# High and low parts of stationary weights stored as alternating words of one tile

## What is computed

```python
def swiglu(h, w_gate, w_up, w_down):
    return (jax.nn.silu(h @ w_gate) * (h @ w_up)) @ w_down

for l in range(DEPTH):
    h = rms_norm(x, ffn1_norm[l])
    x = x + 0.5 * swiglu(h, ffn1_w_gate[l], ffn1_w_up[l], ffn1_w_down[l])
    h = rms_norm(x, mix_norm[l])
    proj = h @ w_in[l]                     # 1024 -> 3080 columns
    # dilated window attention (4 heads of 64), multiscale pooling (256 channels),
    # gated DeltaNet (4 heads of 128, short convolution, chunks of 64)
    ...
    x = x + jnp.concatenate([ya, yb, yc], axis=-1) @ w_out[l]
    h = rms_norm(x, ffn2_norm[l])
    x = x + 0.5 * swiglu(h, ffn2_w_gate[l], ffn2_w_up[l], ffn2_w_down[l])
return rms_norm(x, final_norm)
```

## Time and profile before

| | before |
|---|---|
| median of three runs | 1030.73 us |
| the three runs | 1030.73, 1031.29, 1030.73 us |
| span of the profiled execution | 1029.2 us |
| TensorE busy | 1018.1 us, 99%, 6482 matmuls |
| TensorE weight loads busy | 887.9 us, 86% |
| VectorE busy | 738.5 us, 72% |
| ScalarE busy | 603.0 us, 59% |
| GpSimd busy | 210.0 us, 20% |
| read from HBM | 175.05 MB |

### The profile page before, as it was taken

One profiled execution on the slowest core, in us unless ns is written; L12 is line 12 of the kernel. 1 busy time (PEld: TensorE's weight loads), 2 busy tenths in 40 slices (PEclk: granted clock), 3 DMA queues, 4 the chain that ended last, 5 costly groups with the idle time before them and its releaser, 6 DMA issues.

```text
span 1029.2 us, 19004 instructions
## 1 busy us (share of the span) xinstructions
PE 1018.1 (99%) x6482; PEld 887.9 (86%) x6482; DVE 738.5 (72%) x1204; ACT 603.0 (59%) x1101; POOL 210.0 (20%) x248
## 2 busy tenths in 40 slices
PE   9999999999999999999999999999999999999996
PEld 7888888899988888888888888889999888888885
DVE  6677666798776866666777666678986877666665
ACT  6555555776655655555675555558675575555554
POOL 2867111100400211111111111110014003111111
PEclk9999999999999999999999999999999999999999
DMA  7966666584124666666747666665732238666661
GB/s 246 281 201 188 185 192 190 138 247 153 63 63 123 192 197 187 193 190 184 205 136 211 184 184 188 192 171 164 226 103 66 88 95 266 185 189 196 184 184 41
DMA packets 249881, 176.79 MB, mean 172 GB/s; under 512 B 5875, under 2 KB 235400, under 8 KB 249704
## 3 DMA queue, kind: packets, MB, share of 16 engines
q1 hardware_dynamic: 248800, 174.35, 57.2%
q0 software_dynamic: 400, 1.43, 0.4%
q10 hardware_dynamic: 632, 0.34, 0.1%
HBM read 175.05 MB, written 1.05 MB: 171 GB/s over the span
## 4 chain that ended last, share of the span: by engine, by line
PE 95%; DVE 2%; ACT 2%; issue 0%; DVEq 0%; POOL 0%; POOLq 0%; ACTq 0%
PE bank L742 30%; PE bank L745 16%; PE bank L726 13%; PE bank L727 13%; PE bank L728 13%; PE bank L786 1%; PE bank L1138 1%; PE bank L1125 1%; PE bank L1061 1%; PE bank L751 1%; ACT big L1455 1%; DVE X L1894 1%; PE bank L793 1%; ACT X L1462 1%; DVE Wl L1852 0%; ACT L1567 0%
## 5 line engine op out<-in xcount | busy, mean ns | idle before, releaser
L1852 DVE TENSOR_TENSOR Wl<-raw,Wh 128x1024 fp32r<-128x1024 f32 x324 | 413.8, 1285 | 77.7 <-ACT Wh L1391 77.6
L1391 ACT ACTIVATE Wh<-raw 128x1024 fp32r<-128x1024 f32 x323 | 330.5, 1054 | 84.1 <-PE bank L728 82.2
L742 PE MATMUL bank<-X,Wh 128*128 128x512 f32 x1344 | 336.8, 393 | 0.0
L742 PEld LDWEIGHTS bank<-X,Wh 128*128 128x128 f32 x1344 | 246.8, 188 | 48.9
L745 PEld LDWEIGHTS bank<-X,Wl 128*128 128x128 f32 x1344 | 182.9, 189 | 14.3 <-DVE Wl L1852 0.3
L609 POOL TENSOR_TENSOR gact<-gact,pooled 128x256 f32<-128x256 f32 x85 | 73.8, 868 | 575.7 <-DVE gact L1951 567.1
L745 PE MATMUL bank<-X,Wl 128*128 128x256 f32 x1344 | 187.2, 282 | 0.0
L726 PE MATMUL bank<-Wh,aH 128*128 128x512 f32 x336 | 132.9, 395 | 0.0
L727 PE MATMUL bank<-Wl,aH 128*128 128x512 f32 x336 | 131.9, 392 | 0.0
L728 PE MATMUL bank<-Wh,aL 128*128 128x512 f32 x336 | 131.5, 391 | 0.0
L1506 ACT ACTIVATE dec<-bank 128x256 f32<-128x256 f32 x88 | 33.6, 382 | 118.6 <-PE bank L745 118.5
(11 more groups left out here) (319 smaller groups left out, 1291.7 us busy)
## 6 DMA issues: line engine op xcount, KB each, us to landing
raw<-in_ffn_w_gate SPq DMA_DIRECT2D x88, 512.0 KB, 3.8
raw<-in_ffn_w_up SPq DMA_DIRECT2D x88, 512.0 KB, 3.7
raw<-in_ffn_w_down SPq DMA_DIRECT2D x88, 512.0 KB, 4.3
raw<-in_w_in SPq DMA_DIRECT2D x48, 512.0 KB, 4.3
raw<-in_w_out SPq DMA_DIRECT2D x16, 512.0 KB, 3.5
cst<-in_consts POOLq DMA_DIRECT2D x1, 1200.0 KB, 6.2
xr<-in_x SPq DMA_DIRECT2D x2, 512.0 KB, 4.2
out_x<-big SPq DMA_DIRECT2D x3, 256.0 KB, 2.7
```

The source lines that it names most:

```text
L742: nc.tensor.matmul(b[:, :], piece(Wh, s)[:, k, :], X[:, k, :, :], start=k == 0, stop=False)
L1391: return nc.scalar.activation(Wh[:, s, 0:D_MODEL], raw[:, s, :], ACT.Copy).then_inc(hi_cast.sem, 1)
L1852: return nc.vector.tensor_tensor(Wl[:, s, 0:D_MODEL], raw[:, s, :], Wh[:, s, 0:D_MODEL].bitcast(F32), ALU.subtract).then_inc(lo_cast.sem, 1)
```

## The change

`Wh` and `Wl` become one tile `W` with slots of twice the length, 8448 bytes apart. For row pieces and for the pieces that are moving operands, high and low still stand in two contiguous halves of the slot. For column pieces that are stationary operands, the high and the low word of a value stand next to each other: the views `woven` and `column` read and write every second word. `aH` and `aL` become one tile `A` with alternating high and low words for all tiles of the FFN. `hi` and `lo` get an argument that says which of the two layouts a piece has (`is_column` in the mixer, the first two of three slots in an FFN). The matmuls, casts, loads, waits and their order on each engine stay as they are, and both versions take the same amount of memory.

```diff
@@ -196,11 +196,11 @@
         X = sb("X", [P, KT, 2, SEQ], F32R)
         Xh, Xl = X[:, :, 0, :], X[:, :, 1, :]
         raw = sb("raw", [P, SLOTS, D_MODEL])
-        Wh = sb("Wh", [P, SLOTS, KT * WITH_GATES], F32R)
-        Wl = sb("Wl", [P, SLOTS, KT * WITH_GATES], F32R)
+        W = sb("W", [P, SLOTS, 2 * KT * WITH_GATES], F32R)
+        Wh, Wl = W[:, :, 0:KT * WITH_GATES], W[:, :, KT * WITH_GATES:]
         gate_raw = sb("gate_raw", [P, DEPTH, KT, GATES])
-        aH = sb("aH", [P, 2, SEQ], F32R)
-        aL = sb("aL", [P, 2, SEQ], F32R)
+        A = sb("A", [P, 2, SEQ, 2], F32R)
+        aH, aL = A[:, :, :, 0], A[:, :, :, 1]
         gact = sb("gact", [P, 2, SEQ])
         hid = sb("hid", [P, 2, SEQ])
         stat = sb("stat", [P, HALVES, 8])
...
@@ -459,6 +459,22 @@
         def piece(t, s):
             return t[:, s, 0:D_MODEL].rearrange("p (k c) -> p k c", k=KT)
 
+        def woven(s, part):
+
+            return W[:, s, 0:2 * D_MODEL].rearrange("p (n h) -> p n h", h=2)[:, :, part]
+
+        def column(s, part, k):
+
+            return woven(s, part)[:, k * P:(k + 1) * P]
+
+        def is_column(i):
+
+            return POS_QK <= i < POS_LATE
+
+        def hidden_of(t, par, c):
+
+            return t[:, par, c * P:(c + 1) * P]
+
         def mix_piece(t, i):
 
             if i in GATE_PIECES:
...
@@ -656,7 +672,7 @@
                         scale_tile(layer, g * 2 + (par + f * TILES), par)
 
             pool.wait_ge(landed[1].sem, 16)
-            nc.gpsimd.tensor_copy(Wh[:, 1, 0:D_MODEL], raw[:, 1, :]).then_inc(up_first.sem, 1)
+            nc.gpsimd.tensor_copy(woven(1, 0), raw[:, 1, :]).then_inc(up_first.sem, 1)
 
             for layer in range(DEPTH):
                 ffn(layer, 0)
...
@@ -731,7 +747,7 @@
 
 
                 for k in range(KT):
-                    m = three(outp, piece(Wh, s)[:, k, :], piece(Wl, s)[:, k, :], Xh[:, k, :], Xl[:, k, :],
+                    m = three(outp, column(s, 0, k), column(s, 1, k), Xh[:, k, :], Xl[:, k, :],
                               k == 0, k == KT - 1)
                 return m
 
...
@@ -739,10 +755,10 @@
 
                 pe.wait_ge(*hi_cast.at(layer, index + 1))
                 for k in range(KT):
-                    nc.tensor.matmul(b[:, :], piece(Wh, s)[:, k, :], X[:, k, :, :], start=k == 0, stop=False)
+                    nc.tensor.matmul(b[:, :], column(s, 0, k), X[:, k, :, :], start=k == 0, stop=False)
                 pe.wait_ge(*lo_cast.at(layer, index + 1))
                 for k in range(KT):
-                    m = nc.tensor.matmul(b[:, SEQ:], piece(Wl, s)[:, k, :], Xh[:, k, :], start=False, stop=k == KT - 1)
+                    m = nc.tensor.matmul(b[:, SEQ:], column(s, 1, k), Xh[:, k, :], start=False, stop=k == KT - 1)
                 return m
 
             def turn_quarter(n, c, b):
...
@@ -903,7 +919,7 @@
 
             def down_quarter(par, c, n, first=False, last=False):
                 s = 3 * par + 2
-                return three(acc[c][n][:, :], aH[:, par, c * P:(c + 1) * P], aL[:, par, c * P:(c + 1) * P],
+                return three(acc[c][n][:, :], hidden_of(aH, par, c), hidden_of(aL, par, c),
                              Wh[:, s, n * NW:(n + 1) * NW], Wl[:, s, n * NW:(n + 1) * NW], first, last)
 
             def down(layer, f, t, par, first=False, index=2):
...
@@ -1387,8 +1403,10 @@
 
         @block.scalar
         def _(act):
-            def hi(s):
-                return nc.scalar.activation(Wh[:, s, 0:D_MODEL], raw[:, s, :], ACT.Copy).then_inc(hi_cast.sem, 1)
+            def hi(s, by_column):
+
+                dst, src = (woven(s, 0), raw[:, s, :]) if by_column else (Wh[:, s, 0:D_MODEL], raw[:, s, :])
+                return nc.scalar.activation(dst, src, ACT.Copy).then_inc(hi_cast.sem, 1)
 
             def hi_mix(layer, i):
                 s = MIX_SLOTS[i]
...
@@ -1409,7 +1427,7 @@
                     act.wait_ge(*(gates_done, ups_done, downs_done)[part].at(layer, tile - 1))
                 else:
                     act.wait_ge(*last_out_use(layer, s))
-                hi(s)
+                hi(s, s % 3 < 2)
 
             def x_ready(layer, n, c, b):
                 if layer == 0 and n == 0:
...
@@ -1848,13 +1866,18 @@
 
         @block.vector
         def _(dve):
-            def lo(s):
-                return nc.vector.tensor_tensor(Wl[:, s, 0:D_MODEL], raw[:, s, :], Wh[:, s, 0:D_MODEL].bitcast(F32),
-                                               ALU.subtract).then_inc(lo_cast.sem, 1)
+            def lo(s, by_column):
+                if by_column:
+                    dst, src, high = woven(s, 1), raw[:, s, :], woven(s, 0)
+                else:
+                    dst, src, high = Wl[:, s, 0:D_MODEL], raw[:, s, :], Wh[:, s, 0:D_MODEL]
+                return nc.vector.tensor_tensor(dst, src, high.bitcast(F32), ALU.subtract).then_inc(lo_cast.sem, 1)
 
             def lo_piece(layer, index, s):
+
+                in_mixer = 0 <= index - MIX_BASE < MIX_PIECES
                 dve.wait_ge(*hi_cast.at(layer, index + 1))
-                lo(s)
+                lo(s, is_column(index - MIX_BASE) if in_mixer else s % 3 < 2)
 
             def lo_mix(layer, i):
                 if i in GATE_PIECES:
...
@@ -2046,11 +2070,11 @@
                 mul_half(left).then_inc(half_mul.sem, 1)
                 sum_half(right).then_inc(usum_done.sem, 1)
                 dve.wait_ge(*half_ah.at(layer, f + 1))
-                low_half(left).then_inc(half_al.sem, 1)
+                low_half(0).then_inc(half_al.sem, 1)
                 dve.wait_ge(*usum_done.at(layer, T))
                 mul_half(right).then_inc(mul_done.sem, 1)
                 dve.wait_ge(*ah_done.at(layer, T))
-                low_half(right).then_inc(al_done.sem, 1)
+                low_half(1).then_inc(al_done.sem, 1)
 
             def take_params(layer):
 
...
```

More of the change, by code:

```diff
@@ L785, in wide @@
                             block_ready(layer, n, j)
-                        nc.tensor.matmul(b[:, :], piece(Wh, s)[:, k, :], X[:, k, :, :], start=j == 0, stop=False,
+                        nc.tensor.matmul(b[:, :], column(s, 0, k), X[:, k, :, :], start=j == 0, stop=False,
                                          skip_group_check=True)
@@ L792, in low @@
                         k = SPLIT_ORDER[j]
-                        m = nc.tensor.matmul(b[:, SEQ:], piece(Wl, s)[:, k, :], Xh[:, k, :], start=False, stop=j == KT - 1,
+                        m = nc.tensor.matmul(b[:, SEQ:], column(s, 1, k), Xh[:, k, :], start=False, stop=j == KT - 1,
                                              skip_group_check=True)
@@ L957, in quarter @@
                         return down_quarter(0, c, n)
-                    t, q = slice(c * P, (c + 1) * P), slice(n * NW, (n + 1) * NW)
+                    q = slice(n * NW, (n + 1) * NW)
                     high, low_part, i = (half_ah, half_al, f + 1) if c == 0 else (ah_done, al_done, (f + 1) * TILES)
                     pe.wait_ge(*high.at(layer, i))
-                    nc.tensor.matmul(acc[c][n][:, :], aH[:, 1, t], Wh[:, 5, q], start=False, stop=False)
-                    nc.tensor.matmul(acc[c][n][:, :], aH[:, 1, t], Wl[:, 5, q], start=False, stop=False)
+                    nc.tensor.matmul(acc[c][n][:, :], hidden_of(aH, 1, c), Wh[:, 5, q], start=False, stop=False)
+                    nc.tensor.matmul(acc[c][n][:, :], hidden_of(aH, 1, c), Wl[:, 5, q], start=False, stop=False)
                     pe.wait_ge(*low_part.at(layer, i))
-                    return nc.tensor.matmul(acc[c][n][:, :], aL[:, 1, t], Wh[:, 5, q], start=False, stop=True)
+                    return nc.tensor.matmul(acc[c][n][:, :], hidden_of(aL, 1, c), Wh[:, 5, q], start=False, stop=True)
                 last_two(quarter_order(*after), ready, quarter, downs_done,
@@ L983, in first_piece @@
                         for k in (2 * p, 2 * p + 1):
-                            nc.tensor.matmul(out, piece(Wh, s)[:, k, :], Xh[:, k, :], start=k == 0, stop=False)
-                            nc.tensor.matmul(out, piece(Wh, s)[:, k, :], Xl[:, k, :], start=False, stop=False)
+                            nc.tensor.matmul(out, column(s, 0, k), Xh[:, k, :], start=k == 0, stop=False)
+                            nc.tensor.matmul(out, column(s, 0, k), Xl[:, k, :], start=False, stop=False)
                     split(POS_QK)
                     for k in range(KT):
-                        m = nc.tensor.matmul(out, piece(Wl, s)[:, k, :], Xh[:, k, :], start=False, stop=k == KT - 1)
+                        m = nc.tensor.matmul(out, column(s, 1, k), Xh[:, k, :], start=False, stop=k == KT - 1)
                     return m
@@ L1092, in z_part @@
                     for k in ks:
-                        m = three(bank[3][:, 0:SEQ], piece(Wh, s)[:, k, :], piece(Wl, s)[:, k, :], Xh[:, k, :], Xl[:, k, :],
+                        m = three(bank[3][:, 0:SEQ], column(s, 0, k), column(s, 1, k), Xh[:, k, :], Xl[:, k, :],
                                   k == 0, k == KT - 1)
```

(15 more changed lines are left out.)

## The result

| | before | after |
|---|---|---|
| median (runs) | 1030.93 us (4) | 1037.59 us (4) |
| lowest and highest | 1030.73, 1031.29 us | 1037.23, 1037.82 us |
| span of the profiled execution | 1029.2 us | 1036.0 us |

Before has one run more here than ahead of the prediction. The ratio is 1.006, with a 95% interval of 1.0048 to 1.0072: the change costs 6.7 us. The forecast was a gain of 28 us. The measured time lies inside the range given (971 to 1042 us), on the other side of no change.

A forecast was written before the change was run, and what follows sets the result against it. TensorE, busy 99% of the span, was taken to bound the kernel through the spacings of 6482 matmuls. Profiled span 1029.2 less 28.4 gained plus 1.5 around the span gave 1002.3 us, range 971 to 1042 us.

The forecast's parts named there:

- Zero for ScalarE: ScalarE's casts that write high halves with a step of two were costed at nothing.
- Rival 3: VectorE's casts with a step cost more and make the kernel slower, 1033 to 1070 us; chance 0.08.
- I take half of the extra, 28.4 us: On the strided TensorE matmuls, the gain taken as half of the 56.7 us possible.
- the extra: FFN matmuls' 12 to 17 ns each above mixer matmuls' spacing, read as weight load and moving stream interfering.
- best case: The whole extra goes on 2416 matmuls of 512 columns and 2128 of 256: 56.7 us gained.
- equal walking speeds: With the step doubled, weight load and moving stream walk at nearer speeds, so reads once apart stay apart.
- 227 and 233 ns on two slots: Same FFN matmuls spaced differently at other addresses, 6 ns apart; taken to show that the extra gives way.
- rival 4: All slots fall into the better or worse pattern seen: 1024.9 or 1036.5 us; chances 0.15 and 0.06.
- Rival 2: Weight loads disturb the moving stream twice as often in strided matmuls: 56.7 us slower, 1087 us; chance 0.19.
- Rival 1: Layout doesn't matter to TensorE: time stays at 1030.7 us; chance 0.18.

The follow-up runs named there:

- half_load: slots_even with seven of eight high gate and up weight loads cut from 128 to 64 columns; 1030.22 us, ratio to before 0.9987.
- slots_even: Kernel before with slots lengthened to 4352 bytes, so column weights lie at offset 0 modulo 256 bytes from X in all slots; 1028.51 us, ratio 0.9973.
- pairs_even: slots_even with words of blocks k and k + 4 alternating in Wh, so only high blocks have a step of two; 1032.81 us, ratio to before 1.0012.
- slots_off64: slots_even with 64 unused bytes ahead of Wh, giving offset 64 modulo 256 bytes from X in all slots; 1025.15 us, ratio to before 0.9935.
- high_pairs: Kernel before with words of blocks k and k + 4 alternating in Wh only, a step of two at offsets 0 and 128; 1034.75 us, ratio 1.0033.

## Why the prediction was wrong

**The bound was right.** TensorE alone sets the time, and the other engines' costs stayed covered, the 77 ns on ScalarE's casts included. Zero for ScalarE was wrong as a duration and right as a price. Rival 3 did not happen with a step of two; with a step of four it did (the waits on line 1879 above).

**The step that failed is "I take half of the extra, 28.4 us".** The extra, 12 to 17 ns over 215.5 ns, was read as the time in which a weight load's reads and the moving stream's reads get into each other's way. From that came both the best case and the idea that equal walking speeds would shrink it. half_load takes 54 ns off the load and nothing off the spacing, so the extra doesn't go by how long the load reads. With the step of two, the high gate and up matmuls moved 4.0 ns apart instead of 7 ns together. The matmuls with 215.5 ns differ from the others in two things at once (operand type and rate of the moving stream), and no layout tried came near their spacing: the lowest mean of any run is 227.4 ns for high gate matmuls and 114.9 ns for low ones.

**What the addresses do was seen and misread.** The 227 and 233 ns on two slots were used as a sign that the extra gives way. Their better use was a question that the code answers: the new slot is 8448 bytes, 33 x 256, so which of the two offsets does the change leave? Offset 0, the one with 227 ns. Of rival 4 that would have been the gain of 5.8 us, and even this was too much: it took the 227 ns of the gate matmuls for all 2416, and slots_even, with all slots at offset 0, gains 2.8 us. The step of two turned just that pattern into 233 ns (slots_even to pairs_even), so that the time came out where rival 4 had put its bad side, 1036.5 us, but from the good offset and by the step; that the numbers agree is luck. This small loss had 0.06 of the chances.

**Rival 2** named the place and the sign: wider spacings of strided matmuls, and the load longer by some ns. Its price, 56.7 us, was built on the same misread extra. The 195 ns are 7 in place of its 47 ns more, and the 256-column matmuls, which should have paid most, paid 0.5 ns.

**The two rules.** The two ports of the Trainium skill ("TensorE: Matmul & The Clock Gate", Part 2, step 1) fit half_load: how long the load reads does not matter to the running matmul. They don't explain the rest: moving `Wh`, `Wl` and what lies behind them by 64 bytes, with the same work, is worth 3.8 thousandths (slots_even to slots_off64). Whether the two reads meet somewhere, or the place of the weights matters by itself, is not shown. The line rule ("SBUF — State Buffer", Door 1: The DMA port swizzle), two accesses to a line of 16 bytes for full rate, fits the durations in the main: 193 to 195 ns with two words of a line used, against 188 with four, and 310 with one. Rival 1, which leaned on it, was 7 us off: the spacings changed although the loads lasted only 5 to 7 ns longer.

**The sum.** The loss is 6.2 us by the ratio of 1.006, 6.7 by the two medians. By the ratios, 1.7 us come with the joint tile, 6.2 with the step in the columns, about -1.8 with the activations' step. That a stepped load at offset 0 widens the high matmuls is shown by pairs_even and by the two slots of high_pairs. Why a load that lasts 5 ns longer costs the gate matmuls 6.4 ns there, and nothing at offset 128, is not: no run looked inside the interplay, and slots_even's own up matmuls change pattern in mid-piece. That cause stays open. How it depends on offsets below 32 bytes was not tried.

## What to carry to other kernels

Where TensorE has no gaps, take the price of a layout from start-to-start distances, and work out the new addresses of both operands before judging a new access pattern: here the place of a tile modulo 256 bytes was worth 6.5 us, as much as the whole change lost. A few bytes of padding are cheap to try, but each place has to be tried: in two tiles and without a step, the five others came out between 3.0 thousandths faster and no change. A step of two float32 words in the stationary column weights cost 4 to 6 us of 1031 at offset 0, a step of four in the high blocks alone about 120, and neither buys speed.

## What was not expected of the hardware

- With identical instructions, the mean distance of 256-column matmuls was 114.9 ns at offset 64 and 119.6 at offset 0, that of 512-column ones 233.4 and 228.9 ns.
- A weight load of 64 columns takes 134 ns and one of 128 takes 188, and the matmuls behind the shorter ones are no closer together (230.4 and 228.9 ns).
- From a step of two words to one of four, a weight load of 128 float32r words went from 193 to 310 ns, a cast on ScalarE that writes with the step from 1130 to 2065 ns and one on VectorE that reads one source with it from 1224 to 2001 ns (medians).
